# A different order and different shares for expert work that is slipped in beside attention and projections

## The reference, cut to what matters

```python
for i in range(2):                       # first block
    h = rms_norm(x, attn_norm[i])
    x = x + (even_mixer(h) if i == 0 else mla_mixer(h))   # attention with its projections
    h = rms_norm(x, ffn_norm[i])
    x = x + peer_ffn(h)                  # see below
x = rms_norm(x, final_norm)
x = second_block(x)                      # four kinds of attention, gates, an MLP

def peer_ffn(x):                         # for each token, 8 heads
    q  = x @ w_q
    # top 16 x top 16 product keys -> 16 experts of 16384 for each head
    u, v = u_tab[expert], v_tab[expert]  # 128 rows of 1024 floats each, for each token
    w  = softmax(top_s) * gelu(dot(u, x))
    return sum(w * v)
```

## Time and profile before

| What | Value |
|---|---|
| median of 3 runs | 2481.71 us (2479.70 to 2483.08) |
| profiled execution, its own time | 2483.28 us |
| its span in the trace | 2481.6 us |
| TensorE / VectorE / ScalarE / GpSimd busy | 75% / 58% / 33% / 25% |
| mean DMA rate over the span | 292 GB/s |
| first to last expert gather issued | 221.2 to 1786.8 us |

### The profile page before, as it was taken

How to read it: one execution, slowest core, us unless ns; L and a number is a source line. 1 busy time by engine, 2 the same in 40 slices (tenths; PEclk the granted TensorE clock), 3 DMA queues, 4 the chain that set the end, 5 groups by cost and what they waited for, 6 DMA issues and landing times.

```text
span 2481.6 us, 20915 instructions
## 1 busy us (share of the span) xinstructions
PE 1859.9 (75%) x6670; PEld 1111.8 (45%) x6670; DVE 1433.0 (58%) x2882; ACT 820.6 (33%) x2089; POOL 611.1 (25%) x527
## 2 busy tenths in 40 slices
PE   6662677777776877777787778777759667987988
PEld 3451234453233462233446322222248555866976
DVE  2337684579765467965446885444444365554644
ACT  1210235223334423332522333333324233442532
POOL 0002332344343344443223454333300000000000
PEclk9685898889999989989888899999979755997999
DMA  7154997899999899999879999999924100433442
GB/s 284 36 193 162 422 392 282 336 421 421 383 405 407 327 421 421 384 401 421 316 275 421 421 384 422 422 422 421 421 90 169 69 1 2 191 149 126 172 168 102
DMA packets 103020, 724.84 MB, mean 292 GB/s; under 512 B 12000, under 2 KB 12768, under 8 KB 17152
## 3 DMA queue, kind: packets, MB, share of 16 engines
q0 software_dynamic: 73824, 537.00, 53.1%
q1 hardware_dynamic: 26928, 179.68, 19.0%
q10 hardware_dynamic: 2160, 6.82, 0.7%
HBM read 722.41 MB, written 1.05 MB: 292 GB/s over the span
## 4 chain that ended last, share of the span: by engine, by line
PE 40%; DVE 23%; DMA 23%; ACT 8%; issue 3%; DVEq 1%; PEldq 0%; POOL 0%; POOLq 0%; ACTq 0%; PEld 0%; SPq 0%
DMA sb_work<-in_peer_uv,sb_expert 19%; PE ps_acc L1232 8%; DVE sb_work L1196 7%; PE bank L423 5%; PE bank L488 3%; PE bank L1072 3%; PE bank L489 3%; PE bank L490 3%; PE bank L667 2%; PE ps_acc L489 2%; PE ps_acc L488 2%; PE ps_acc L490 2%; DMA sb_wring<-in_peer_w_q 2%; DVE sb_x L1204 2%; PE ps_turn L368 2%
## 5 line engine op out<-in xcount | busy, mean ns | idle before, releaser
L1232 PE MATMUL ps_acc<-sb_work,sb_diag 128*128 128x512 f32 x1660 | 855.2, 655 | 332.2 <-ACT sb_diag L1221 283.4
L1795 POOL DMA_INDIRECT sb_work<-in_peer_uv,sb_expert x512 | 605.9, 1183 | 1179.1 <-PE ps_acc L1232 657.1
L1196 DVE CUSTOM_DVE_ANT_0 sb_work<-sb_work,sb_h 128x1024 f32<-128x1024 f32 x512 | 618.4, 1223 | 281.0 <-DMA sb_work<-in_peer_uv,sb_expert 255.5
L1232 PEld LDWEIGHTS ps_acc<-sb_work,sb_diag 128*128 128x128 f32 x1660 | 321.4, 207 | 822.8 <-issue 814.1
L1212 ACT ACTIVATE sb_dots<-sb_dots 128x1 f32<-128x1 f32 x512 | 102.7, 201 | 648.5 <-DVE sb_dots L1196 616.0
L482 DVE TENSOR_TENSOR sb_work_r<-sb_wring,sb_work_r 128x2048 fp32r<-128x2048 f32 (+2 forms) x80 | 168.7, 2130 | 152.2 <-ACT sb_work_r L475 152.2
L475 ACT CAST sb_work_r<-sb_wring 128x2048 fp32r<-128x2048 f32 (+2 forms) x80 | 140.2, 1777 | 118.2 <-PE ps_acc L490 57.3
L423 PE MATMUL bank<-sb_wring,sb_hT 128*128 128x512 f32 (+2 forms) x392 | 157.3, 557 | 23.9 <-DMA sb_wring<-in_hyb_w_in 7.8
L1204 DVE SCALAR_TENSOR_TENSOR sb_x<-sb_work,sb_weight,sb_x 128x1024 f32<-128x1024 f32 x97 | 124.4, 1283 | 83.5 <-ACT sb_weight L1213 83.4
L1221 ACT ACTIVATE sb_diag<-sb_ident,sb_weight 128x128 f32<-128x128 f32 x415 | 166.6, 401 | 13.6
L1213 ACT ACTIVATE sb_weight<-sb_dots,sb_share 128x1 f32<-128x1 f32 x512 | 150.7, 294 | 16.6
(11 more groups left out here) (258 smaller groups left out, 2040.6 us busy)
## 6 DMA issues: line engine op xcount, KB each, us to landing
sb_wring<-in_peer_w_q SPq DMA_DIRECT2D x32, 1024.0 KB, 7.8
sb_wring<-in_hyb_w_in SPq DMA_DIRECT2D x20, 1024.0 KB, 7.6
sb_wring<-in_w_mix SPq DMA_DIRECT2D x18, 1024.0 KB, 4.8
sb_wring<-in_w_gate SPq DMA_DIRECT2D x16, 1024.0 KB, 4.9
sb_wring<-in_w_up SPq DMA_DIRECT2D x16, 1024.0 KB, 4.9
sb_wring<-in_w_down SPq DMA_DIRECT2D x16, 1024.0 KB, 4.8
sb_wring<-in_mla_w_uq SPq DMA_DIRECT2D x12, 768.0 KB, 9.9
sb_wring<-in_hyb_w_out SPq DMA_DIRECT2D x8, 1024.0 KB, 11.0
```

Source lines behind the costliest of these rows:

```text
L1196: e.tensor_tensor_reduce(u, u, h[:, t, :], 1.0, 0.0, ALU.mult, ALU.add, dots[:, i:i + 1]).then_inc(dot_ready, 1)
L1232: last = e.matmul(ps_acc[:, b * 512:(b + 1) * 512], diag[:, number % DIAGS, :], ring[:, n % RING, D + b * 512:D + (b + 1) * 512], start=k ...
L1795: pool.indirect_dma_start(ring[:, n % RING, :], None, a["peer_uv"], bass.IndirectOffsetOnAxis(ap=expert[:, t, n % P:n % P + 1], axis=0)).t ...
```

## The change

Four things are edited. In `attend`, where `ahead` is 0, TensorE turns the last group's probabilities before the items of the group's first point and no longer behind them; ScalarE copies the turned probabilities of the last group first, then makes the exponentials, then does the items of the first point (before: items, exponentials, copies). The two points of each group weigh 9.0 and not 6.0. The points of projections weigh 0.0006 for each chunk and column in place of 0.0017, and those of `route`'s projection 2.5 (four) and 2.0 (one) in place of 7.0 and 4.0. The planner spreads six picks fewer over the points (`HELD_BACK = 6`), which leaves them to `finish_experts`. Groups of the attentions with two score buffers keep their order.

```diff
+HELD_BACK = 6
...
-            return f["first"] + int(weight * min((P - f["first"]) / max(f["weight"], 1.0), RATE))
+            return f["first"] + int(weight * min((P - HELD_BACK - f["first"]) / max(f["weight"], 1.0), RATE))
...
-            points = [point(len(tiles) * chunks * bn * 0.0017, "pe") for _, _, bn, _, _, _ in plan]
+            points = [point(len(tiles) * chunks * bn * 0.0006, "pe") for _, _, bn, _, _, _ in plan]
...
-                plan.append(g | value | {"points": [point(6.0), point(6.0)]})
+                plan.append(g | value | {"points": [point(9.0), point(9.0)]})
...
                     if n + ahead < len(plan):
                         score(plan[n + ahead])
-                    g["points"][0]("pe", e)
                     if n and not ahead:
                         turn_probs(n - 1, plan[n - 1])
+                    g["points"][0]("pe", e)
                     if n:
                         sum_values(n - 1, plan[n - 1])
                     g["points"][1]("pe", e)
...
                 for n, g in enumerate(plan):
-                    g["points"][0]("act", e)
+                    if ahead:
+                        g["points"][0]("act", e)
+                    elif n:
+                        empty_turns(e, n - 1, plan[n - 1])
                     w, k = g["w"], len(g["maps"])
...
                         last.then_inc(from_act.sem if g["kind"] == "diff" else probs_ready.sem, 1)
-                    if n:
+                    if not ahead:
+                        g["points"][0]("act", e)
+                    elif n:
                         empty_turns(e, n - 1, plan[n - 1])
                     g["points"][1]("act", e)
...
-            made = [point(7.0, "pe") for _ in range(4)] + [point(4.0, "pe")]
+            made = [point(2.5, "pe") for _ in range(4)] + [point(2.0, "pe")]
```

## The result

The changed kernel is slower. Its median is 2491.26 us (16 runs, 2483.53 to 2496.50), that of the kernel before 2481.70 us (16 runs). The ratio is 1.0037, with a 95% interval of 1.0026 to 1.0049. I had forecast 2488, slower, with 2461 to 2508 as the range.

A forecast was written before the change was run, and what follows sets the result against it. It held that the first block, bound by DMA transfers, can shorten only by less idle DMA time. Feed 1 +1, feeds 2 and 3 +2.5 each, the rest 0: together +6, giving 2488 us, range 2461 to 2508.

The forecast's parts named there:

- My sum: Whole kernel: feed 1 +1, feeds 2 and 3 +2.5 each, together +6 us; 2484 to 2500 given 0.42.
- ahead of attention: Stages before each attention shorten with fewer picks: -17 us in `hybrid(1)`, -13 in each latent.
- in attention: The three attentions grow: +28 us in `hybrid(1)`, +25 in each latent, with 22 and 31 as bounds.
- behind it with the finish: Output projection to `finish_experts`: -10 us in `hybrid(1)`, -9.5 in each latent, including +6.5 for the finish.
- The order: In attention: TensorE's second pick waits some 5.7 us for a diagonal behind the exponentials; some 10 us of each attention's growth.
- my formula: One attention group of 256 keys: 9.7 + 1.7 + 6.25 x 1.72 + 3.5 = 25.7 us for 7.25 picks.
- The drain: ScalarE's table switches in attention: the skill's rule would add 33 us over twelve groups; the prediction took none.
- The rival with the drain: Table drains count in the attention groups: 2488 + 33 = 2521 us; chance 0.02.
- Idle DMA time: First block shortens only by less idle DMA time; in the attentions it stays near 75 us.
- Transfers bind all that lies outside attention: Stretches outside attention fall by their bounds: feed 1 -5, the others -8 each, 2461 us; chance 0.18.
- No wait is left in attention: Attention groups take 18 us, attentions no longer than now, the +78 falls away: 2410 us; chance 0.06.

The follow-up runs named there:

- the first experiment: The kernel before with only the new order of steps in the one-bank attentions, all shares as before: 2485.5 us, ratio 1.0019 to the kernel before.
- the shares alone: The changed kernel with the old order in attention, its new points and six held-back picks kept: 2470.4 us, ratio 0.9962 to the kernel before.

## Why the prediction was right, point by point

**The direction and the size.** My sum was +6, the spans differ by +9.7. By term, measured from the profiles against what I took: ahead of attention -16.5, -16.2 and -14.6 (I had -17, -13, -13); in attention +21.0, +26.9 and +14.9 (+28, +25, +25); behind it with the finish -3.7, -1.8 and -0.2 (-10, -9.5, -9.5). That the total came out near is luck: I had put 15 us too much into the attentions, taken 23 us too much off behind them and 4 too little off ahead of them, and these errors stood against each other. What was right is the mechanism in attention, and the direction.

**The order.** The mechanism was right: the wait ahead of the values goes, one pick can be done, and the second waits for a diagonal behind the exponentials. I had the wait at 5.7 us (9.7 less the 3.8 of work is 5.9); it is 4.77. A group of eight picks takes 26.0 us and one of seven 23.1, where my formula gives 26.9 and 25.2. Two prices in it were too high, and one was at the low end. I took the values at 3.5 us from the earlier trace rows, where they ran right behind an idle of 5 us; behind picks they take 1.89. And the table load for the exponentials now begins at 1208.51, before the softening has ended at 1209.66, so 1.15 of its 1.28 us are off the path; I had all of it behind. Against that, the picks behind the wait lose 1.7 to 2.8 us, where I took 1.7. I had put 10 us of each attention down to the order; against the shares alone they are 13.8, 13.1 and 6.2 in the profiles, the profile of the shares alone being of the shortest of its seven executions, and 19 us in all by the ratios. On the old shares the order is a near tie, as the first experiment shows; the prediction had no term for that case.

**The drain.** The load of 1208.51 ends at 1209.79 and the exponential starts at 1209.80: nothing stands between them, and nothing between the copies, which end at 1208.48, and the load. The Trainium skill ("ScalarE: Activation LUTs", "What ACT_TABLE_LOAD costs") puts a drain of about 1380 ns on top of each load. The trace does not agree with it here either. The rival with the drain, 2521, is out by the measured 2491.

**Ahead of attention.** The projection of `hybrid(1)` fell to 45.2 us, not 41: TensorE waits in it for weights for 5.1 us, at 396 GB/s. The latents fell by 15 to 16 us, more than my 13: VectorE's waits for rows, 13.8 us in `latent(1)`, fell to 1.2. The idle DMA time that I expected there is there: 110.8 x (1 - 391/421) = 7.9 us for 2.7.

**Behind attention.** This is the term that I sized most wrongly. I gave the finish +6.5 on the ground that some of the rows would have landed; it took +11.0, since the ranking is bound by transfers up to its end (422 GB/s) and leaves nothing in the slots. That six picks held back alone make no difference shows the same: here the gap at the hand-over is filled at the price of waiting for the same bytes one stage later. The query projection fell by 7.7 us and not by 10, and the DMA engines idle in it for 7.8 us: five picks and the weights do not keep them busy beside it.

**Idle DMA time.** The prediction set out to count it and then summed lengths of stages; by its own measure, length times (1 - rate/421), the account is this. In the attentions it fell from 75 us to 22.5 + 17.5 + 24.6 = 65, where I expected it to stay near 75. In the six stretches outside them it rose from 39 to 58: 13 of that ahead of the attentions (11 to 25), 6 behind them (27 to 33), where the gap at the end of the ranking is gone but the query projection of feed 3 idles for 7.8. A rise of 19 against a fall of 10 is the loss of 9.7, within the rounding of the rates. The change takes picks from stages that kept the DMA engines busy, and its order lets the attentions use only part of them. With the diagonals ahead of the exponentials the same shares leave 9.9 us idle in the attentions, 55 less.

**The rivals.** "Transfers bind all that lies outside attention" was half right ahead of attention and wrong behind it. "No wait is left in attention" was wrong for this order, and nearly right for the one that makes the diagonals first: there the first two attentions move 413 and 414 GB/s, and the kernel comes to 2426, within 16 us of the 2410 that I had worked out for that case; waits of 8.8 us for diagonals are left in the last attention.

## What to carry to other kernels

When one engine's work is slipped in beside another stage, look for the item that the first engine can't do without the second, and count how many of them are ready when the wait begins: a long step that is moved ahead of them on the second engine (here the exponentials with two table loads) moves the wait and does not remove it. In this kernel it paid to put what feeds the busy engine first, and behind it the step that is needed only at the next turn of the loop. And test an order and the shares that came with it one by one: here the points of attention alone gained 0.8%, the order cost 0.75% on the new shares, and one swap of lines on top of it gained 2.4%.

## What the runs showed of the hardware

The products with the values (16 matmuls of 64 columns as the trace counts them) took 3.30 and 3.65 us right behind an idle of 5 us, and 1.89 us behind picks in the group shown. Three picks behind an idle of 4.77 us took 8.22 us in one group and 7.58 in another, 5.39 behind an idle of 0.79; two picks took 5.37 in a third, and 3.67 behind an idle of 0.48. So the picks behind one such wait lost 1.7 to 2.8 us. The granted clock of the first two attentions with the same 31 picks was 0.85 with the wait and 0.98 with waits under 3 us. ScalarE's table load for the exponentials started right behind the copies, 1.15 us before the operand that they wait for was ready.
